# A fused encoder layer: which projection steps run beside the loading of x, and who spreads the cosines

## The chip, the cores and the metric

The kernel runs on one Trainium2 chip. Its eight cores run the same program, each on one element of the batch (2048 rows of 1024 channels), with no exchange between them. The metric is the device time of the slowest core, in microseconds (us). Engines are named PE (TensorE, matmuls and transposes), ACT (ScalarE), DVE (VectorE), POOL (GpSimd) and SP (SyncE, which here only issues DMAs). Each engine works through a queue of its own in program order; semaphores make it wait for others.

## The reference, cut to what matters

```python
h = rms_norm(x, norm_mix_pre)                      # 2048 x 1024, one norm per row
proj = h @ w_in
u_pool, q, k, v, g_pool, g_attn = split(proj)      # 512, 3 x 1536, 2 x 1024 channels
q, k = apply_rope(q, cos, sin), apply_rope(k, cos, sin)
for gi, (window, dil) in enumerate(((128, 1), (512, 4), (2048, 16))):
    o, lse = dilated_window_attention(q[g], k[g], v[g], dil, radius=64)   # 8 heads a group
# groups merged by softmax of lse; branch A: windowed means of u_pool
mix = (sigmoid(g_pool) * y_pool + sigmoid(g_attn) * y_attn) @ w_out
x = x + rms_norm(mix); x = x + rms_norm(SwiGLU(rms_norm(x)))
```

The change touches only the first lines: the norm of x, the projection to v and to q and k, and the rotation by cosine and sine.

## The kernel before, in words

**Tiles of x.** x comes in 16 tiles of 128 rows (512 KB each), over SP's queue into a ring of six buffers (`xring`). For tile i, `p1_s1` issues the load, `p1_s1b` squares the tile on ACT with a sum per row and makes 1/rms by a Ln and an Exp on one column, `p1_s2` multiplies on DVE by 1/rms and by the gain row g0 (one SCALAR_TENSOR_TENSOR, bf16 out, ring `hbf` of three), `p1_s3` transposes it with eight PE instructions into one bank of PSUM, and `p1_s4` copies the bank on DVE into hT. `p1_iter(t)` is one turn of this pipeline: in turn t the later stages come first, for tiles t-3, t-2 and t-1, then the square of tile t, then the load of tile t+5.

**Steps of projection.** After each `p1_iter(t)` the program puts up to 9 units of projection on PE (`run(9.0, ...)`), taken from the list `ready` when their turn has come (`pro(t)`). A step is 8 units. A v step (`v_step(w, n2)`) makes two 128-row tiles of v for the slab w: 16 matmuls of 256 columns against the weights `Wv[w % 2]`, one ACT copy out. Slab w holds 256 channels of v of head group w % 3. A q or k step (`qk_step(u, m, tb)`) makes 512 rows of q or k for unit u: 8 matmuls of 512 columns, then DVE multiplies the bank by the sines into bf16 and by the cosines in place, PE adds the rotated part with one more 512-column matmul about 11 units later, and ACT copies the result out (one copy for q, two for k). Before the change, `ready` holds the eight v steps of slab 0 and the eight q and k steps of unit 0. All sixteen are emitted by the end of the pipeline, behind turn 19.

**Then the attention.** 160 attention groups follow, each with a score step, an Exp, a mask multiply and a value step. Between them `pace(i)` says how many units of further projection (the list `jobs`, sorted by due group) are emitted per group: 18.4 for each of the first 14 groups.

**The other queues.** POOL fills constants in memory (`vones`, `kzero`), issues the weight loads that convert float32 to bf16 (`issue_v`, `issue_qk`) and, before the change, copies cosine and sine rows, which arrive in 32 partitions, over to the other 96 (eight copies of 1024 float32 columns, the line L622). Its waits on tiles of x (`tk._waits("pool", ...)`) hold back the weight loads. SP issues the loads of x and the constants; before it issues tile i it waits for tile i-3 to have landed, and for the buffer to be free.

The tables of order below name PE's rows so: L176 is a transpose, L170 with 128x256 a matmul of a v step, L173 a matmul of 512 columns of a q or k step, L170 with 128x512 the rotation.

## Time and profile before

| | us |
|---|---|
| median of 3 runs | 1144.59 (1143.5 to 1144.81) |
| profiled execution | 1146.5 |
| its span, slowest core (core 3) | 1145.0 |
| spans of the eight cores | 1139.3 to 1145.0 |
| PE busy in the span | 1084.6 (95%) |
| DVE, ACT, POOL busy | 523.2, 474.7, 96.2 |

The span runs from the first to the last instruction of a core; the profiled execution's time is 1.5 us longer than it. A timeline row says when a merged row of instructions starts, how long it takes, and in brackets how long the engine sat idle before it and which event ended that. A row of a stretch gives the stretch, its length, the busy time and number of instructions of PE, PE's weight loads, DVE, ACT and POOL, then the TensorE clock that was granted (1.00 is full speed), the busy share of the DMA engines and the GB/s that they moved. Of the DMA queues, q1 (hardware) is SP's and q0 (software) POOL's. A busy PE is not always a fast PE: the same instruction can take longer at a lower clock, so durations are compared too.

### The profile page before, as it was taken

To read this page: it belongs to the slowest core of one execution; us is meant where nothing else is said; L and a number is where in the kernel's file an instruction comes from. 1 tells how busy PE (TensorE), PEld (TensorE's weight loads), DVE (VectorE), ACT (ScalarE), POOL (GpSimd) and SP (SyncE) were. 2 spreads that over 40 slices of the span, in tenths; PEclk is the share of its full clock that TensorE was granted. 3 is DMA by queue.
4 is the path that set the end of the run, shared out by engine and by line. 5 is a ranking of instruction groups with operands and counts; after the bars stand their busy time and mean duration, and the time that the engine had idled before them with its cause. 6 is when DMAs were issued, how large, how long until landed. Compare 5 with 4: busy or idle time off the path is not lost.

```text
span 1145.0 us, 19739 instructions; the slowest of 8 cores (1139.3 to 1145.0 us)
## 1 busy us (share of the span) xinstructions
PE 1084.6 (95%) x6896; PEld 591.3 (52%) x6896; DVE 523.2 (46%) x817; ACT 474.7 (41%) x904; POOL 96.2 (8%) x181
## 2 busy tenths in 40 slices
PE   2799998989999999999999999999999999999995
PEld 1586564557665696444444444444444444444442
DVE  3835567765557765443436777212112111222221
ACT  3744476577565666322224878211111111211111
POOL 5620000000000000002000000111111000000000
PEclk9899999999999999999999999999999999999998
DMA  8852211121121403716004741554545210333321
GB/s 216 213 88 38 37 20 19 20 38 20 20 47 21 65 2 58 147 19 92 1 1 145 242 142 61 92 75 75 81 77 79 39 19 1 111 111 110 111 92 56
DMA packets 32017, 83.07 MB, mean 73 GB/s; under 512 B 4016, under 2 KB 4272, under 8 KB 31792
## 3 DMA queue, kind: packets, MB, share of 16 engines
q0 software_dynamic: 18768, 36.31, 20.7%
q1 hardware_dynamic: 13152, 45.49, 12.0%
q8 instruction: 58, 0.95, 0.3%
q14 instruction: 39, 0.32, 0.1%
HBM read 101.32 MB, written 16.78 MB: 103 GB/s over the span
## 4 chain that ended last, share of the span: by engine, by line
PE 81%; ACT 6%; DVE 6%; issue 4%; DMA 2%; ACTq 0%; DVEq 0%; SPq 0%; POOL 0%
PE ps L173 67%; PE ps L170 13%; ACT arena L184 6%; DVE arena L187 2%; DMA arena<-x 2%; DVE arena L190 2%; DVE arena L201 1%; ACT arena L255 1%; DVE ps L187 0%; PE ps L176 0%; DVE arena L197 0%; ACTq L68 0%; DVEq L68 0%; ACT L255 0%; ACT arena L592 0%
## 5 line engine op out<-in xcount | busy, mean ns | idle before, releaser
L173 PE MATMUL ps<-arena 128*128 128x512 bf16 (+2 forms) x4304 | 925.3, 368 | 9.7 <-ACT arena L184 4.5
L173 PEld LDWEIGHTS ps<-arena 128*128 128x128 bf16 x4304 | 412.6, 98 | 472.0 <-issue 17.3
L184 ACT ACTIVATE arena<-ps 128x512 bf16<-128x512 f32 (+5 forms) x578 | 352.6, 619 | 611.5 <-PE ps L173 498.0
L187 DVE TENSOR_TENSOR arena<-ps,arena 128x512 bf16<-128x512 f32 (+3 forms) x332 | 223.8, 677 | 433.7 <-PE ps L173 326.8
L170 PE MATMUL ps<-arena 128*128 128x256 bf16 (+5 forms) x2336 | 220.5, 239 | 7.6 <-DVE ps L187 3.2
L170 PEld LDWEIGHTS ps<-arena 128*128 128x128 bf16 x2336 | 168.4, 105 | 30.0 <-issue 12.9
L187 DVE TENSOR_TENSOR arena<-arena 128x512 bf16<-128x512 bf16 (+2 forms) x208 | 108.2, 524 | 78.7 <-ACT arena L184 69.6
L184 ACT ACTIVATE arena<-arena 128x1 f32<-128x1 f32 (+3 forms) x161 | 86.0, 538 | 36.8 <-DMA arena<-x 15.8
L190 DVE SCALAR_TENSOR_TENSOR arena<-arena 128x1024 bf16<-128x1024 f32 (+2 forms) x49 | 63.1, 1290 | 24.5 <-ACT arena L184 21.0
L187 DVE TENSOR_TENSOR ps<-ps,arena 128x512 f32<-128x512 f32 x96 | 67.2, 700 | 10.3 <-DVE arena L187 0.5
L176 PE MATMUL ps<-arena 128*128 128x128 bf16 x256 | 21.9, 235 | 29.8 <-DVE arena L190 28.7
L176 PEld LDWEIGHTS ps<-arena 128*128 128x128 bf16 x256 | 17.8, 105 | 37.9 <-issue 34.9
L201 DVE CAST arena<-ps 128x256 bf16<-128x256 f32 (+1 forms) x54 | 28.5, 528 | 10.2 <-PE ps L170 6.9
L210 POOL DMA_DIRECT2D arena<-w_fg x22 | 12.1, 549 | 216.3 <-PE ps L173 216.3
L197 DVE TENSOR_SCALAR arena<-arena 128x1 f32<-128x1 f32 (+1 forms) x28 | 7.5, 268 | 46.7 <-ACT arena L184 46.7
L210 POOL DMA_DIRECT2D arena<-w_qk x24 | 12.8, 537 | 160.8 <-PE ps L170 101.5
L190 DVE SCALAR_TENSOR_TENSOR arena<-ps,arena 128x1024 f32<-128x1024 f32 x16 | 20.5, 1280 | 6.2 <-ACT arena L184 6.1
L210 POOL DMA_DIRECT2D arena<-w_gt x16 | 8.5, 530 | 165.6 <-PE ps L173 96.0
L368 POOL MEMSET arena<- 64x2048 bf16 x8 | 14.4, 1798 | 0.9
L210 POOL DMA_DIRECT2D arena<-w_fu x22 | 11.8, 537 | 21.3 <-PE ps L173 21.3
L253 POOL MEMSET arena<- 128x1 f32 x32 | 2.4, 138 | 130.7 <-DVE arena L190 121.6
L195 DVE TENSOR_SCALAR arena<-ps,arena 128x512 bf16<-128x512 f32 x16 | 11.8, 743 | 0.3
(25 smaller groups left out, 96.3 us busy)
## 6 DMA issues: line engine op xcount, KB each, us to landing
arena<-x SPq DMA_DIRECT2D x32, 512.0 KB, 5.3
y<-arena SPq DMA_DIRECT2D x31, 512.0 KB, 2.9
arena<-y SPq DMA_DIRECT2D x16, 512.0 KB, 4.2
arena<-w_qk POOLq DMA_DIRECT2D x24, 256.0 KB, 4.1
arena<-w_fg POOLq DMA_DIRECT2D x22, 256.0 KB, 4.2
arena<-w_fu POOLq DMA_DIRECT2D x22, 256.0 KB, 5.4
arena<-w_fd POOLq DMA_DIRECT2D x11, 512.0 KB, 7.9
arena<-w_gt POOLq DMA_DIRECT2D x16, 256.0 KB, 4.3
```

The lines of the kernel that those rows point to most:

```text
L170: tk.op("pe", lambda e: e.matmul(out, lhsT=lhsT, rhs=rhs, start=start, stop=stop, skip_group_check=True), reads, writes, mark)
L173: tk.op("pe", lambda e: e.matmul(out, lhsT=lhsT, rhs=rhs, start=start, stop=stop), reads, writes, mark)
L176: tk.op("pe", lambda e: e.transpose(out, in_, ident), reads, writes, mark)
L184: tk.op("act", lambda e: e.activation(out=out, in_=in_, func=func, **kw), reads, writes)
L187: tk.op(eng, lambda e: e.tensor_tensor(out=out, in0=in0, in1=in1, op=op), reads, writes)
L190: tk.op("dve", lambda e: e.scalar_tensor_tensor(out=out, in0=in0, scalar=scalar, in1=in1, op0=op0, op1=op1), reads, writes)
L195: tk.op("dve", lambda e: e.tensor_scalar(out=out, in0=in0, scalar1=s1, scalar2=None, op0=op0), reads, writes)
L197: tk.op("dve", lambda e: e.tensor_scalar(out=out, in0=in0, scalar1=s1, scalar2=s2, op0=op0, op1=op1), reads, writes)
L201: tk.op("dve", lambda e: e.tensor_copy(out=out, in_=in_), reads, writes)
L210: tk.dma(qeng, key, lambda e: e.dma_start(out=out, in_=in_), reads, writes)
L255: tk.op("act", lambda e: e.activation(out=st[:, 1:2], in_=st[:, 0:1], func=AF.Ln, bias=epsb, scale=1.0 / D), (r, "epsb"), (r,))
L368: tk.op("pool", lambda e, o_=KT[s_][h_][z, :]: e.memset(o_, 0.0), (), (("Kz", s_), "pms"))
```

## The change

It does these things, all ahead of or within the loading of x:

1. The gain row is loaded into 32 partitions instead of 128, and two DVE copies spread it. Tile 0 of x is the first DMA that SP issues; the constants c_pk come third instead of first. The cosine and sine rows are asked for behind tile 9 instead of tile 3.
2. Up to four tiles of x are in flight instead of three (tile i waits for tile i-4). Turn t now holds the stages of tiles t-4, t-3 and t-2, and the square of tile t; each stage but the square is one turn later.
3. From tile 4 on, one Ln and one Exp serve two tiles. The square's unused output goes to a buffer of its own (`sqj`) instead of into `hbf`.
4. `ready` holds the v steps of slabs 0 and 1 while x is loading; q and k steps of unit 0 come from turn 17 on. Slab 1 (group 1, dilation 4) stores its tiles of v by row range first, so that two steps are possible from every four tiles of x; the value step of the attention reads them at the new place (`nv`).
5. DVE instead of POOL spreads the cosines, two copies in each of the turns 13 to 16. POOL asks for the weights of slab 0 behind tile 2 (was 1), of slab 1 behind tile 4 (was 14), of unit 0 behind tile 10 (was 3).
6. The eight v steps of slab 1 are gone from `jobs`, and `pace` gives 14.0 units for each of the first 14 groups.

```diff
         def after_x(i):
             if i == 0:
-                DMA("sp", "c2", g0, gains[0:1, :].partition_broadcast(128), writes=("g0",))
-            if i == 3:
+                DMA("sp", "c2", g0[0:32, :], gains[0:1, :].partition_broadcast(32), writes=("g0",))
+                DMA("sp", "c0", f32v(O_SM, 128), c_pk[:, 0:128], writes=("smbf",))
+            if i == 9:
...
         def p1_s1(i):
-            if i >= 2:
-                tk._waits("sp", tk._deps((("xr", max(i - 3, 0) % 6),), ()))
+            if i >= 4:
+                tk._waits("sp", tk._deps((("xr", (i - 4) % 6),), ()))
...
         def p1_s1b(i):
-            ACT(hbf[i % 3], xring[sl], AF.Square, ...)
+            ACT(sqj, xring[sl], AF.Square, ...)
+            a = i
+            if i >= 4:
+                if i % 2 == 0:
+                    return
+                a = i - 1
...
-        P1 = (p1_s1b, p1_s2, p1_s3, p1_s4)
-        for i in range(5):
+        P1 = ((0, p1_s1b), (2, p1_s2), (3, p1_s3), (4, p1_s4))
+        for i in range(6):
             p1_s1(i)
+        for n_ in (32, 64):
+            VCOPY(g0[n_:2 * n_, :], g0[0:n_, :], reads=("g0",), writes=("g0",))
...
-            ready = sorted([(2 * n2 + 5, 0, n2, f_) for n2, f_ in enumerate(w_steps(0))] +
-                           [(4 * (n_ % 4) + 8, 1, n_, f_) for n_, f_ in enumerate(u_steps(0))])
+            ready = sorted([(2 * n2 + 6, 0, n2, f_) for n2, f_ in enumerate(w_steps(0))] +
+                           [(4 * (n2 // 2) + 8, 1, n2, f_) for n2, f_ in enumerate(w_steps(1))] +
+                           [(max(4 * (n_ % 4) + 9, 17), 2, n_, f_) for n_, f_ in enumerate(u_steps(0))])
...
+                if 13 <= t < 17:
+                    q_ = t - 13
+                    for n_ in (32, 64):
+                        c_ = arena[:, O_CS + q_ * 1024:O_CS + (q_ + 1) * 1024]
+                        VCOPY(c_[n_:2 * n_, :], c_[0:n_, :], reads=(("cs", q_),), writes=(("cs", q_),))
...
-            add(w_steps(1), 0, 4)
...
-                    return 18.4
+                    return 14.0
```

PE at the start of the program, before: four transposed tiles, a v step, and then, from tile 6 on, v steps and q or k steps by turns between the tiles.

```order
L176 MATMUL ps<-arena 128x128 x32
L170 MATMUL ps<-arena 128x256 x16
L176 MATMUL ps<-arena 128x128 x16
L170 MATMUL ps<-arena 128x256 x16
L176 MATMUL ps<-arena 128x128 x8
L173 MATMUL ps<-arena 128x512 x9
L176 MATMUL ps<-arena 128x128 x8
L173 MATMUL ps<-arena 128x512 x7
L170 MATMUL ps<-arena 128x512
L170 MATMUL ps<-arena 128x256 x4
L176 MATMUL ps<-arena 128x128 x8
L170 MATMUL ps<-arena 128x256 x12
```

PE at the same place in the changed kernel:

```order
L176 MATMUL ps<-arena 128x128 x32
L170 MATMUL ps<-arena 128x256 x16
L176 MATMUL ps<-arena 128x128 x16
L170 MATMUL ps<-arena 128x256 x18
L176 MATMUL ps<-arena 128x128 x8
L170 MATMUL ps<-arena 128x256 x18
L176 MATMUL ps<-arena 128x128 x8
L170 MATMUL ps<-arena 128x256 x18
L176 MATMUL ps<-arena 128x128 x8
L170 MATMUL ps<-arena 128x256 x10
L176 MATMUL ps<-arena 128x128 x8
```

From the seventh tile on, each tile of transposes is followed by 18 or 10 matmuls of v steps, and none of a q or k step. Of the first x18, 16 matmuls belong to slab 0 and the last two to slab 1.

PE in the changed kernel around the last two tiles (the two L176 rows are the transposes of tiles 14 and 15), to the first q and k steps:

```order
L170 MATMUL ps<-arena 128x256 x18
L176 MATMUL ps<-arena 128x128 x8
L170 MATMUL ps<-arena 128x256 x18
L176 MATMUL ps<-arena 128x128 x8
L170 MATMUL ps<-arena 128x256 x12
L173 MATMUL ps<-arena 128x512 x16
L170 MATMUL ps<-arena 128x512
L173 MATMUL ps<-arena 128x512 x10
L170 MATMUL ps<-arena 128x512
```

All q and k steps of unit 0 stand behind the last tile's transposes.

DVE in the turns of the cosines; before, one turn with a q or k step in it and the next ones (the second row is the multiply for tile 11):

```order
L201 COPY arena<-ps 128x8x128 [waits pe]
L190 SCALAR_TENSOR_TENSOR arena<-arena 128x1024 [waits x5,act]
L187 TENSOR_TENSOR arena<-ps,arena 128x512 [waits pe,pool]
L187 TENSOR_TENSOR ps<-ps,arena 128x512 [waits dve]
L201 COPY arena<-ps 128x8x128
L190 SCALAR_TENSOR_TENSOR arena<-arena 128x1024 [waits x0,act]
L187 TENSOR_TENSOR arena<-ps,arena 128x512 [waits pe]
L187 TENSOR_TENSOR ps<-ps,arena 128x512 [waits dve]
```

and in the changed kernel (the first row is the multiply for tile 11, the 32x1024 and 64x1024 copies are the cosines):

```order
L190 SCALAR_TENSOR_TENSOR arena<-arena 128x1024 [waits x5,dve]
L201 COPY arena<-arena 32x1024 [waits c40]
L201 COPY arena<-arena 64x1024 [waits dve]
L201 COPY arena<-ps 128x8x128 [waits pe]
L190 SCALAR_TENSOR_TENSOR arena<-arena 128x1024 [waits x0,act]
L201 COPY arena<-arena 32x1024 [waits c41]
L201 COPY arena<-arena 64x1024 [waits dve]
L201 COPY arena<-ps 128x8x128 [waits pe]
L190 SCALAR_TENSOR_TENSOR arena<-arena 128x1024 [waits x1]
```

The multiplies by sine and cosine (TENSOR_TENSOR) have left the turns of the tiles, and two copies stand in each of four turns.

POOL, from its first fill on, before:

```order
L360 MEMSET arena 128x32x64
L368 MEMSET arena 64x2048 [waits pool] x2
L210 DMA arena<-w_v 128x2048 [waits x1]
L210 DMA arena<-w_qk 128x1024 [waits x3]
L210 DMA arena<-w_qk 128x1024
L622 COPY arena<-arena 32x1024 [waits c40,pool]
L622 COPY arena<-arena 64x1024 [waits pool]
L622 COPY arena<-arena 32x1024 [waits c41,pool]
```

and now:

```order
L368 MEMSET arena 128x32x64
L368 MEMSET arena 128x32x64 [waits pool]
L376 MEMSET arena 64x2048 [waits pool] x2
L210 DMA arena<-w_v 128x2048 [waits x2]
L376 MEMSET arena 64x2048 [waits pool] x2
L210 DMA arena<-w_v 128x2048 [waits x4]
L376 MEMSET arena 64x2048 [waits pool] x4
L210 DMA arena<-w_qk 128x1024 [waits x4]
L210 DMA arena<-w_qk 128x1024
L210 DMA arena<-w_qk 128x1024 [waits x2]
```

The load of slab 1 stands behind the landing of tile 4 (the second wait on x4 is that of tile 10, in the same buffer), and the copies of cosines are gone.

## Rows read from the trace of the kernel before

**Rows 1.** Spans of the cores, and the granted clock of each
```profile
core 1: 1139.3 us, clock 0.995
...
core 3: 1145.0 us, clock 0.992
```

**Rows 2.** Stretches of core 3, with busy times, clock, DMA share and GB/s
```profile
5.00:8.00 3.00, 0.00 (x0) 0.00 (x0) 0.00 (x0) 0.00 (x0) 1.70 (x1) 1.00 1.05 374
8.00:14.00 6.00, 1.06 (x9) 0.85 (x10) 2.77 (x3) 3.29 (x8) 0.66 (x1) 1.00 0.89 237
14.00:22.00 8.00, 1.97 (x16) 1.47 (x16) 3.79 (x4) 3.30 (x8) 2.92 (x4) 1.00 1.03 242
22.00:30.00 8.00, 4.72 (x32) 3.62 (x32) 3.22 (x5) 3.41 (x9) 7.22 (x7) 0.91 0.93 219
30.00:36.00 6.00, 3.97 (x28) 3.25 (x29) 5.47 (x5) 3.60 (x9) 5.64 (x4) 0.56 0.83 263
80.00:100.00 20.00, 20.00 (x152) 13.02 (x151) 9.36 (x16) 7.78 (x14) 1.06 (x2) 1.00 0.24 40
```

**Rows 3.** Timeline of core 3, TensorE: start, duration, instruction, idle before and releaser
```profile
23.07 2.90 PE L170 MATMUL ps<-arena 128*128 128x256 bf16 x16
...
32.84 3.13 PE L170 MATMUL ps<-arena 128*128 128x256 bf16 x16
...
45.36 1.91 PE L170 MATMUL ps<-arena 128*128 128x256 bf16 x16
47.11 0.61 PE L176 MATMUL ps<-arena 128*128 128x128 bf16 x8
47.56 2.11 PE L173 MATMUL ps<-arena 128*128 128x512 bf16 x9
49.50 0.61 PE L176 MATMUL ps<-arena 128*128 128x128 bf16 x8
...
60.81 0.61 PE L176 MATMUL ps<-arena 128*128 128x128 bf16 x8
```

**Rows 4.** The same view of core 1
```profile
20.73 3.57 PE L170 MATMUL ps<-arena 128*128 128x256 bf16 x16 [1.22 <-DMA arena<-w_v]
...
54.96 0.61 PE L176 MATMUL ps<-arena 128*128 128x128 bf16 x8
```

**Rows 5.** Waits of core 3 in 0 to 62 us: total, times, longest
```profile
PE ps L176 <- DVE arena L190: 27.9, 10, 11.7
```

**Rows 6.** Timeline of core 3, ScalarE: square of tile 4, all of tile 5
```profile
24.93 1.06 ACT L184 ACTIVATE arena<-arena 128x1024 bf16<-128x1024 f32 x1 [4.53 <-DMA arena<-x]
...
28.06 1.06 ACT L184 ACTIVATE arena<-arena 128x1024 bf16<-128x1024 f32 x1 [1.30 <-DMA arena<-x]
29.02 0.19 ACT L184 ACTIVATION_READ_ACCUMULATOR arena<-arena 128x1 f32 x1
29.30 0.29 ACT L308 ACTIVATE arena<-arena 128x1 f32<-128x1 f32 x1
29.68 0.20 ACT L184 ACTIVATE arena<-arena 128x1 f32<-128x1 f32 x1
```

**Rows 7.** DMAs issued in 8 to 14 us, core 3: size, us to landing
```profile
arena<-w_v POOLq DMA_DIRECT2D x1, 512.0 KB, 11.7
```

**Rows 8.** DMA queues in 14 to 22 us: packets, MB, share
```profile
q1 hardware_dynamic: 426, 1.41, 69.3%
q0 software_dynamic: 141, 0.52, 34.0%
```

**Rows 9.** ScalarE by form, 0 to 62 us: count, busy, mean ns
```profile
L184 ACT ACTIVATE arena<-ps 128x512 bf16<-128x512 f32 x8 | 4.8, 597 | 4.6 <-PE ps L170 4.5
```

**Rows 10.** Groups of VectorE by form, whole span
```profile
L190 DVE SCALAR_TENSOR_TENSOR arena<-arena 128x1024 bf16<-128x1024 f32 x32 | 42.4, 1326 | 19.6 <-ACT arena L184 19.6
...
L201 DVE COPY arena<-ps 128x1024 bf16<-128x1024 bf16 x16 | 10.9, 680 | 0.0
L197 DVE TENSOR_SCALAR arena<-arena 128x512 f32<-128x512 f32 x12 | 5.0, 420 | 2.2 <-ACT arena L184 2.2
```

More of the change, by code:

```diff
@@ L306, in p1_s1b @@
             r = ("st1", i)
-            ACT(hbf[i % 3], xring[sl], AF.Square, reads=(("xr", sl), r), writes=(("hbf", i % 3), r), accum_out=st1[:, 0, i:i + 1])
-            tk.op("act", lambda e: e.activation(out=st1[:, 1, i:i + 1], in_=st1[:, 0, i:i + 1], func=AF.Ln, bias=epsb, scale=1.0 / D),
-                  (r, "epsb"), (r,))
-            ACT(st1[:, 2, i:i + 1], st1[:, 1, i:i + 1], AF.Exp, reads=(r,), writes=(r,), scale=-0.5)
+            ACT(sqj, xring[sl], AF.Square, reads=(("xr", sl), r), writes=("sqj", r), accum_out=st1[:, 0, i:i + 1])
+            a = i
[3 more added lines that the diff above has]
+                a = i - 1
+            rr = tuple(("st1", q_) for q_ in range(a, i + 1))
+            tk.op("act", lambda e: e.activation(out=st1[:, 1, a:i + 1], in_=st1[:, 0, a:i + 1], func=AF.Ln, bias=epsb, scale=1.0 / D),
+                  rr + ("epsb",), rr)
+            ACT(st1[:, 2, a:i + 1], st1[:, 1, a:i + 1], AF.Exp, reads=rr, writes=rr, scale=-0.5)
         def p1_s2(i):
@@ L328, in p1_s4 @@
             VCOPY(hT[:, :, i * 128:(i + 1) * 128], pb, reads=(("ps", k),), writes=(("hT", i),))
-        P1 = (p1_s1b, p1_s2, p1_s3, p1_s4)
-        for i in range(5):
+        P1 = ((0, p1_s1b), (2, p1_s2), (3, p1_s3), (4, p1_s4))
+        for i in range(6):
             p1_s1(i)
+        for n_ in (32, 64):
+            VCOPY(g0[n_:2 * n_, :], g0[0:n_, :], reads=("g0",), writes=("g0",))
         def p1_iter(t):
-            for stg in reversed(range(4)):
+            for stg, fn in reversed(P1):
                 if 0 <= t - stg < NT:
-                    P1[stg](t - stg)
-            if t + 5 < NT:
-                p1_s1(t + 5)
+                    fn(t - stg)
+            if 6 <= t + 4 < NT:
+                p1_s1(t + 4)
         HT_ALL = tuple(("hT", i) for i in range(NT))
@@ L610, in grp_step, with wait_x @@
                 yield 1.0
+            def wait_x(i):
+                tk._waits("pool", tk._deps((("xr", i % 6),), ()))
             vones(0)
+            vones(1)
             kzero(0)
-            tk._waits("pool", tk._deps((("xr", 1),), ()))
+            wait_x(2)
             issue_v(0)
-            tk._waits("pool", tk._deps((("xr", 3),), ()))
-            issue_qk(0)
-            for q_ in range(4):
-                for n_ in (32, 64):
-                    src = arena[0:n_, O_CS + q_ * 1024:O_CS + (q_ + 1) * 1024]
-                    dst = arena[n_:2 * n_, O_CS + q_ * 1024:O_CS + (q_ + 1) * 1024]
-                    tk.op("pool", lambda e, o_=dst, i_=src: e.tensor_copy(out=o_, in_=i_), (("cs", q_),), (("cs", q_), "pms"))
@@ L628, in pro @@
             def pro(t):
                 return ready.pop(0)[3] if ready and ready[0][0] <= t else None
-            for t in range(NT + 4):
+            for t in range(NT + 5):
                 p1_iter(t)
                 clock[0] += 2.0
-                run(9.0, lambda: pro(t))
-                if t == 15:
-                    tk._waits("pool", tk._deps((("xr", 14 % 6),), ()))
-                    issue_v(1)
+                if 13 <= t < 17:
[3 more added lines that the diff above has]
+                        VCOPY(c_[n_:2 * n_, :], c_[0:n_, :], reads=(("cs", q_),), writes=(("cs", q_),))
+                run(9.0, lambda: pro(t))
+                if t == 10:
+                    wait_x(10)
+                    issue_qk(0)
+                if t == 14:
+                    wait_x(14)
@@ L638, in _rest @@
                     issue_qk(1)
-                    kzero(2)
-                    kzero(3)
                     issue_qk(2)
@@ L653, in _rest @@
             tk.inherit(tuple(("oat", j, hh) for j in range(4) for hh in range(2)),
-                       tuple(("hbf", i) for i in range(3)) + ("g0",))
+                       tuple(("hbf", i) for i in range(3)) + ("g0", "sqj"))
             def qwin(g, n):
```

16 lines of the change are left out of this document (10 added, 6 removed).

## The prediction, made before the changed kernel ran

> **What bounds the kernel now.** I read the spans of the cores first. The slowest, core 3, ends 5.7 us behind core 1 [rows 1], though both run the same program. Then I looked for a place in the two timelines of PE where the cores differ and after which they don't: the transposes of the last tile of x start at 60.81 us on core 3 [rows 3] and at 54.96 on core 1 [rows 4]. That is 5.85 apart, the whole difference. So the loading of x decides which core is slowest, and it is this stage that the change rewrites.
>
> How much of that stage is lost? I count what PE has executed ahead of tile 15, by the order of before: 15 tiles of transposes, 96 matmuls of v steps, 41 of q and k steps, 4 rotations. Full-speed prices come from start-to-start distances on core 3: a v step of 16 matmuls 47.11 - 45.36 = 1.75 (0.109 each), a tile's transposes 47.56 - 47.11 = 0.45, and 9 matmuls of 512 columns 49.50 - 47.56 = 1.94 (0.216 each) [rows 3]. Sum: 15 x 0.45 + 96 x 0.109 + 45 x 0.216 = 6.75 + 10.5 + 9.7 = 27.0 us. Lost before tile 15: 60.81 - 27.0 = 33.8 us on core 3, 28.0 on core 1. This "loss" (PE idle, or slower than full speed) is the quantity that the change can alter: the matmuls of the whole program stay the same in number and shape, and from tile 15 on PE has no gap to speak of (20.00 busy of 20.00 between 80 and 100 us [rows 2]).
>
> What makes the loss has two parts. Until 30 us it is DMA: the engines are 89 to 105% busy and move 374, 237, 242 and 219 GB/s in the four stretches to 30 us [rows 2], and ACT starts the squares of tiles 4 and 5 only when they land, at 24.93 and 28.06 [rows 6]. Behind that, PE waits for the multiply of DVE ahead of its transposes, 27.9 us in ten waits over the stage [rows 5], because sine and cosine multiplies stand in DVE's queue between the tiles. Core 3 was also granted less clock between 22 and 36 us (a mean of 0.91 and 0.56, from 2.4 GHz down to the 1.2 GHz level in part of it), after stretches with PE busy 1.97 of 8 and 4.72 of 8 us [rows 2]; its second v step took 3.13 us there instead of 1.91 [rows 3].
>
> **The change part by part.** The order of the changed kernel has 15 tiles of transposes and 180 v matmuls ahead of tile 15: 6.75 + 180 x 0.109 = 26.4 us of full-speed work. So I need the time T at which tile 15's transposes start; the new loss is T - 26.4. Two paths lead to T on core 3.
>
> *The DMA path.* What has to be moved until x15 has landed: 16 tiles of 0.524 MB (8.39), gains into 32 rows 0.13 (was 0.52), c_pk 0.06, cosines 0.52, the slabs 0 and 1 0.52 each, the weights of unit 0 0.52: 10.67 MB. From 8 to 30 us before moved 6 x 0.237 + 8 x 0.242 + 8 x 0.219 = 5.1 MB in 22 us, 0.232 MB/us, with full engines [rows 2]. At that rate, less 1.8 us for the 3 us at 374 GB/s, and starting at 4 to 5 us as before, x15 lands at 4.5 + 46 - 1.8 = 48.7. By queue, 1.41 MB of SP took 69.3% of 8 us, 3.9 us per MB, and 0.52 MB of POOL 34.0%, 5.2 us per MB [rows 8]; 9.1 x 3.9 + 1.57 x 5.2 = 43.7, so 48.2 without the faster start and 46.4 with it. From landing to transposes: tile 5 took 1.82 from the start of its square to the end of its Exp (28.06 to 29.88 [rows 6]), the multiply takes 1.33 [rows 10], and I add 0.3 for hand-overs, 3.5 in all. T is 50 to 52 by this path.
>
> *The PE path.* PE's queue now has the first two matmuls of slab 1 ahead of tile 6, and everything behind them is in order. Slab 1 is asked for when tile 4 has landed. The five tiles, gains, c_pk and parts of slab 0 and tile 5 are some 3.4 MB, which at before's pace (1.1 MB in 5 to 8 us [rows 2] and about 0.25 earlier, then 0.232 per us) is 16.8 us, against 24.93 before. A load of v took 11.7 us from issue to landing in that crowd [rows 7]; so PE starts at 28.5, or, if the 5.4 MB up to slab 1 are counted instead, at 25.5. I take 27. Done by then: 6 tiles and 32 matmuls, 2.7 + 3.5 = 6.2 us. Left until tile 15: 20.2. T = 47.2 with no stall.
>
> Stalls on that path. ACT per two tiles: 2 x (1.06 + 0.19) + 0.29 + 0.20 [rows 6], two copies of v at 0.60 [rows 9], 4.2 us, where PE needs 4.4 (64 matmuls and four tiles are 8.8 per four turns): just hidden. With a Ln and an Exp for each tile it would be 4.7 and not hidden, 0.3 per two tiles over five pairs, so the pairing is worth about 1.5 us, already in the 47.2. DVE per tile: multiply 1.33 + copy 0.68 [rows 10], 2.0, hidden. In the four turns 13 to 16 it also has two cosine copies. The trace has no such copy on DVE. From below stands the nearest float32 operation with one input, 0.42 for 512 columns; from above the two-input one at 1.33 for 1024 [rows 10]. I take 0.7, nearest to the first, as the one-input form is about half as costly per column. Four turns are then 4 x (2.0 + 1.4) = 13.6 against PE's 8.8, 4.8 too long, less what the multiplies run ahead of PE, which I put at most of one turn, 1.8: 3 us. With 0.42 it is 1, with 1.33 about 8. If the DMA path is late anyway, part of it hides there. One slow v step more at the start, 3.13 - 1.91 = 1.2. PE path: T = 51.4.
>
> The Trainium skill (VectorE: DVE Perf Modes, "The perf-mode tier table") says that a float32 copy in SBUF runs at 2x, a tensor_tensor at 1x. By its fixed 151 cycles and 0.96 GHz a copy of 1024 would be an estimated 0.69 us, and the sum as above; at 1x the other end. The 0.42 of the 512-column row agrees with 2x.
>
> I take T = 50.7 on core 3: loss 24.3, gain 33.8 - 24.3 = 9.5. On core 1, whose first v step waited for its slab until 20.73 [rows 4] against 23.07, DMA is about 3 us ahead: T = 47.7 to 48.5, loss 21.7, gain 6.3.
>
> The rest. *POOL's eight copies* vanish; POOL was waited for by nothing that paces. *c_pk third*: its transposes need it only after tile 0; nothing. *g0 by two copies*: 1.4 us on DVE beside tile 0's square and statistics (1.8 [rows 6]), behind a quarter of the bytes; hidden, and it ends in DMA time anyway. *Cosines asked for behind tile 9*: SP's four issues delay tile 10 by about 2.4 us, with three tiles in flight; hidden unless DMA idles. *issue_qk(0) behind tile 10*: landing near 45, needed behind tile 15; if it came 10 us late PE would wait 3. *Unit 0 behind tile 15*, then unit 1: sixteen q and k steps nearly in a row; 1.4 of DVE per 1.95 of PE, hidden, bounded by -1 to +2 us. *Slab 1 out of jobs, 14.0 for 18.4*: 64 units less over 14 groups is 4.6 per group; neither gain nor loss beyond 1 us.
>
> Sum against the profiled execution: 1145.0 - 9.5 = 1135.5 of span, 1137.0 with the 1.5 around it. The runs shown have a median 1.9 below that execution, so their slowest core had not quite core 3's bad start; I give them the mean of 9.5 and 6.3, 8.0: 1144.6 - 8.0 = 1136.6.
>
> **The rivals.** (a) *The crowd is thinner than I think.* Landing of slab 1 at 24 and no stall by the cosines: T = 45 to 46, gain 13 to 14, 1131. For it: DMA moved 374 GB/s for a while [rows 2]. Against: 10.67 MB still have to come. The Trainium skill (DMA: Bandwidth & Descriptors, "Queues, rings and completion order") has each DMA engine take turns between queues, packet by packet, so a slab would get half the rate beside x and land in about 4.5 us once it starts. Here q0 moved 141 packets against 426 of q1 in 8 us, a quarter [rows 8]: not that.
>
> (b) *DVE takes PE's place.* Cosine copies at 1.33, or turns that were hidden by less than I think: 5 us more, gain 3, 1141.5. For it: DVE is what PE waits for now [rows 5]. Against: 0.42 [rows 10].
>
> (c) *DMA was the bound and stays it*: with two slabs ahead of x the rate falls to 0.2 MB/us, x15 lands near 55, T = 58, loss 32: gain 2, within the noise, 1142.5 to 1144. Against: between 30 and 36 us 263 GB/s with 83% [rows 2].
>
> (d) *Slower: the slab gates x.* Slab 1's two matmuls stand ahead of tile 6. While they wait, no transposes run, hbf's three buffers fill, the multiplies stop, x's ring fills and the loads stop. Then T = (landing of slab 1) + 20.2 + 4.2. It equals the old loss at T = 60.2, so from a landing at 35.8 on the change loses. A slab that takes twice 11.7 us lands at 40: 4 us slower, 1149. Four tiles in flight instead of three speak for it, the order in which bytes are asked for against it.
>
> **How the numbers follow.** Forecast 62%; (a) 13%, (b) 11%, (c) 7%, (d) 7%. The range takes in (a) to its middle, the bounds of the copies and most of (b): 1131.5 to 1142. A measurement here tells about 0.2%, 2.3 us, from no change. Faster by more: forecast, (a), (b) and a little of (c), 0.86; within, most of (c): 0.08; slower 0.06.
>
> **What would show it.** After: tile 15's transposes near 50 on the slowest core; the square of tile 5 before 22 us; the first x18 row waiting for DMA of w_v until 25 to 29; cosine copies of about 0.7; 263 GB/s or so until the end of x; no sine multiply before tile 15; and spans of the cores nearer to each other. Wrong if PE's sum of waits for the multiply stays near 27.9 past 25 us, if tile 15 starts later than 54, or if gaps appear between 60 and 120 us.

## The result, and the profile after

The changed kernel took 1141.38 us (median of 8 runs) against 1145.09 for the kernel before on the same chip, a ratio of 0.9967 with a 95% interval of 0.9955 to 0.9978. So it is faster by 3.7 us, 0.3%, where I forecast 8.0 and gave 1131.5 to 1142.0 as the range; the forecast gain was more than twice the measured one. One of the eight runs, with four cores at a lower granted clock (0.88 to 0.90), took 1250.2 and is not in the ratio. The profiled execution took 1141.0, its slowest core 1139.5.

The spans of the cores, as in [rows 1]: all eight now end between 1138.1 and 1139.5. Core 3 gained 5.9 us, core 1 only 1.2.

```profile
core 1: 1138.1 us, clock 0.996
...
core 3: 1139.1 us, clock 0.995
...
core 7: 1139.5 us, clock 0.995
```

The stretches of [rows 2] on core 3:

```profile
5.00:8.00 3.00, 0.00 (x0) 0.00 (x0) 1.21 (x1) 1.61 (x4) 2.88 (x2) 1.00 0.97 289
8.00:14.00 6.00, 2.02 (x16) 1.55 (x16) 5.61 (x6) 4.46 (x12) 3.50 (x4) 1.00 0.99 294
14.00:22.00 8.00, 3.06 (x22) 2.31 (x23) 6.08 (x7) 4.00 (x9) 7.61 (x6) 1.00 0.98 223
22.00:30.00 8.00, 7.06 (x63) 5.98 (x62) 3.52 (x4) 4.02 (x11) 1.45 (x1) 1.00 1.02 250
30.00:36.00 6.00, 6.00 (x68) 5.54 (x67) 4.54 (x6) 4.49 (x9) 1.05 (x2) 1.00 1.03 336
80.00:100.00 20.00, 19.00 (x125) 10.62 (x124) 14.23 (x23) 10.09 (x18) 4.40 (x4) 1.00 0.43 61
```

The reader sees the transfers run as full as before, PE busy earlier (7.06 of 8 us between 22 and 30, where it was 4.72), and a granted clock of 1.00 in every stretch. Matmuls at the very start are slow all the same: the first v step below took 3.57 us for 16 matmuls, where 1.91 is usual [rows 3]. That is about half the pace at a granted clock of 1.00, and what causes it stays open; core 1 had the same 3.57 before [rows 4]. Between 80 and 100 us PE now has two small waits of about 0.5 us, where it had none (one of them, for ACT, was there before at 74.55); the rest of the program is nonetheless about as long as before, as shown below. PE's timeline, to set beside [rows 3]:

```profile
20.96 3.57 PE L170 MATMUL ps<-arena 128*128 128x256 bf16 x16 [3.41 <-DMA arena<-w_v]
...
25.54 2.13 PE L170 MATMUL ps<-arena 128*128 128x256 bf16 x18
...
35.56 2.13 PE L170 MATMUL ps<-arena 128*128 128x256 bf16 x18
...
47.24 0.61 PE L176 MATMUL ps<-arena 128*128 128x128 bf16 x8 [1.78 <-DVE arena L190]
...
50.78 0.61 PE L176 MATMUL ps<-arena 128*128 128x128 bf16 x8 [0.97 <-DVE arena L190]
...
54.20 0.61 PE L176 MATMUL ps<-arena 128*128 128x128 bf16 x8 [0.85 <-DVE arena L190]
```

The first row is the first v step, which waits 3.41 us for slab 0. The second is the second step with the first two matmuls of slab 1 behind it, the third such a row further on (2.13 us for 18 matmuls, at full speed). The last three rows are the transposes of tiles 13, 14 and 15. Tile 15 starts at 54.20, where the forecast had 50.7. Between tiles 13, 14 and 15 lie 3.54 and 3.42 us, though PE has only 2.4 us of work per tile; in each case it waits for the multiply of DVE. The sum of PE's waits up to 62 us, beside [rows 5]:

```profile
PE ps L176 <- DVE arena L190: 19.1, 9, 11.6
...
PE ps L170 <- DMA arena<-w_v: 3.4, 1, 3.4
```

Of the 19.1 us (27.9 before), 11.6 are the wait for tile 0 and 1.8 the two ahead of tiles 2 and 3; 5.6 lie behind 25 us, 3.6 of them ahead of tiles 13 to 15 in the rows above. What DVE does in these last turns, on core 7, the slowest: two cosine copies (one row, x2), the tile copy, the multiply, and again.

```profile
47.99 1.47 DVE L201 COPY arena<-arena 32x1024 f32<-32x1024 f32 x2
49.49 0.69 DVE L201 COPY arena<-ps 128x1024 bf16<-128x1024 bf16 x1
50.10 1.28 DVE L190 SCALAR_TENSOR_TENSOR arena<-arena 128x1024 bf16<-128x1024 f32 x1
51.41 1.47 DVE L201 COPY arena<-arena 32x1024 f32<-32x1024 f32 x2
52.91 0.69 DVE L201 COPY arena<-ps 128x1024 bf16<-128x1024 bf16 x1
53.52 1.28 DVE L190 SCALAR_TENSOR_TENSOR arena<-arena 128x1024 bf16<-128x1024 f32 x1
```

and PE beside it:

```profile
48.10 0.61 PE L176 MATMUL ps<-arena 128*128 128x128 bf16 x8 [1.84 <-DVE arena L190]
...
51.52 0.61 PE L176 MATMUL ps<-arena 128*128 128x128 bf16 x8 [0.85 <-DVE arena L190]
```

DVE's rows follow one another without a gap, every 3.42 us (47.99, 51.41, ...), and a tile's transposes start right after a multiply ends. Two cosine copies take 1.47, so one is 0.735; the forecast had 0.7.

How far back does this chain reach? On core 3 (DVE for tiles 10 and 14, ACT for tile 15):

```profile
37.11 1.28 DVE L190 SCALAR_TENSOR_TENSOR arena<-arena 128x1024 bf16<-128x1024 f32 x1 [1.54 <-ACT arena L184]
...
45.17 1.06 ACT L184 ACTIVATE arena<-arena 128x1024 bf16<-128x1024 f32 x1 [1.61 <-DMA arena<-x]
...
46.80 0.20 ACT L184 ACTIVATE arena<-arena 128x2 f32<-128x2 f32 x1
...
49.36 1.28 DVE L190 SCALAR_TENSOR_TENSOR arena<-arena 128x1024 bf16<-128x1024 f32 x1
```

DVE waits for the last time ahead of the multiply of tile 10, at 37.11. From there its queue runs without a wait, and tile 15's transposes start 17.1 us later (17.0 to 17.2 on all eight cores). The last tile of x is not part of this chain. Its square starts at 45.17, as soon as it has landed, and the Exp for tiles 14 and 15 ends at 47.00; but DVE reaches the multiply of tile 14 only at 49.36, 2.4 us later (2.2 to 3.4 over the cores). So in the changed kernel the transfers are done in time, and DVE is late.

One pair of numbers describes every kernel of this study: T, the start of tile 15's transposes, and the rest, a core's span less its T. Before, T is 54.96 to 60.81 over the eight cores (mean 56.97) and the rest 1084.2 to 1084.5. In the changed kernel T is 53.35 to 54.95 (mean 54.25) and the rest 1084.2 to 1084.9 (mean 1084.6 for 1084.3). The start of tile 6's transposes went from 29.95 to 35.80 (eight cores) to 28.61 to 29.75. From tile 6 to tile 15 it was 25.0 us on most cores before and is 24.0 to 25.6 after: nothing was won there. So, by these numbers, the change made the late cores as early as the good ones, and little more.

### The profile page after: what moved, and what is told of

Read it like the earlier page. It is cut to its first block, busy times and chain, and to the rows that moved or that the text cites. A ratio compares the mean times of both kernels' runs of the same rounds, so it can differ in the third digit from the quotient of the medians.

```text
span 1139.5 us, 19711 instructions; the slowest of 8 cores (1138.1 to 1139.5 us)
## 1 busy us (share of the span) xinstructions
PE 1084.6 (95%) x6896; PEld 590.0 (52%) x6896; DVE 532.1 (47%) x827; ACT 471.2 (41%) x892; POOL 87.7 (8%) x173
## 4 chain that ended last, share of the span: by engine, by line
PE 79%; DVE 7%; ACT 6%; issue 4%; DMA 2%; ACTq 0%; DVEq 0%; SPq 0%; POOL 0%; POOLq 0%
PE ps L173 67%; PE ps L170 12%; ACT arena L184 6%; DVE arena L190 3%; DMA arena<-x 2%; DVE arena L187 2%; DVE arena L201 1%; ACT arena L255 0%; DVE ps L187 0%; DVE arena L197 0%; ACTq L68 0%; DVEq L68 0%; ACT L255 0%; SPq L210 0%; ACT arena L600 0%
## 5 line engine op out<-in xcount | busy, mean ns | idle before, releaser
L173 PEld LDWEIGHTS ps<-arena 128*128 128x128 bf16 x4304 | 412.8, 98 | 472.8 <-issue 17.2
L184 ACT ACTIVATE arena<-arena 128x1 f32<-128x1 f32 (+4 forms) x155 | 84.3, 550 | 29.8 <-DMA arena<-x 9.8
L176 PE MATMUL ps<-arena 128*128 128x128 bf16 x256 | 21.2, 231 | 20.3 <-DVE arena L190 19.5
L176 PEld LDWEIGHTS ps<-arena 128*128 128x128 bf16 x256 | 17.4, 104 | 27.6 <-issue 25.2
L201 DVE COPY arena<-ps 128x1024 bf16<-128x1024 bf16 x16 | 11.0, 687 | 6.0 <-PE ps L176 5.8
```

What stands on the lines that cost most here:

```text
L173: tk.op("pe", lambda e: e.matmul(out, lhsT=lhsT, rhs=rhs, start=start, stop=stop), reads, writes, mark)
L176: tk.op("pe", lambda e: e.transpose(out, in_, ident), reads, writes, mark)
L184: tk.op("act", lambda e: e.activation(out=out, in_=in_, func=func, **kw), reads, writes)
L201: tk.op("dve", lambda e: e.tensor_copy(out=out, in_=in_), reads, writes)
```

## The experiments

Each was taken in turn with the kernel before on one chip, which gives the ratio. The chip was not the same for all: e_late, e_pool, e_third and e_unpair ran on one, e_late2, a_oldsteps, b_oldfront and p_early on a second, e_mix, p_three and p_gains on a third. So between groups the ratios are compared, and where their intervals overlap no difference is claimed. All numbers of T and of the rest are read from the eight cores' timelines of one profiled execution.

| kernel | median us | ratio to before (95%) | T, mean (lowest to highest) | rest, mean |
|---|---|---|---|---|
| changed kernel | 1141.4 | 0.9967 (0.9955 to 0.9978) | 54.2 (53.4 to 55.0) | 1084.6 |
| e_late | 1142.7 | 0.9977 (0.9966 to 0.9988) | 50.5 (49.3 to 51.6) | 1088.4 |
| e_pool | 1138.3 | 0.9938 (0.9924 to 0.9951) | 50.6 (49.8 to 51.7) | 1084.7 |
| e_third | 1144.2 (one run) | | 57.1 (56.1 to 58.7) | 1084.1 |
| e_unpair | 1141.4 | 0.9966 (0.9954 to 0.9978) | 53.9 (52.8 to 55.8) | 1085.1 |
| e_late2 | 1139.6 | 0.9947 (0.9933 to 0.9961) | 50.5 (49.1 to 52.7) | 1086.1 |
| a_oldsteps | 1145.3 | 0.9997 (0.9987 to 1.0007) | 57.4 (55.6 to 59.0) | 1084.1 |
| b_oldfront | 1145.7 | 0.9999 (0.9989 to 1.0009) | 53.2 (50.1 to 56.1) | 1086.7 |
| p_early | 1139.2 | 0.9943 (0.9927 to 0.9960) | 51.2 (49.5 to 52.9) | 1084.5 |
| e_mix | 1140.1 | 0.9955 (0.9941 to 0.9970) | 51.1 (49.6 to 52.4) | 1085.0 |
| p_three | 1141.0 | 0.9969 (0.9956 to 0.9982) | 52.4 (50.2 to 55.0) | 1084.5 |
| p_gains | 1138.7 | 0.9945 (0.9925 to 0.9965) | 51.6 (50.3 to 53.0) | 1084.0 |

**e_late: the copies behind the last tile.**

```diff
-                if 13 <= t < 17:
-                    q_ = t - 13
+                for q_ in {17: (0, 1), 18: (2,), 19: (3,)}.get(t, ()):
```

> The changed kernel, with the eight cosine copies moved out of the turns 13 to 16 into the turns 17 to 19, behind the last multiply of a tile. Theory D (DVE took PE's place: its queue of tile copy 0.68 + multiply 1.28 + two cosine copies 1.47 = 3.42 us per tile in four turns is the chain that leads to tile 15): without them PE goes on at 2.42 or 1.55 us per tile from the transposes of tile 12 on, tile 15's transposes start at 50.5 instead of 54.2 to 55 us, and the kernel takes 1137.5, that is 3.5 to 4.4 us less than the changed kernel's 1141.4 and about 0.9935 of the kernel before. Theory X (the loading of x and of the slabs is what the end of the stage waits for, DVE only fills the time): tile 15's transposes stay within 1 us of 54.5 and the time at 1141. Rival P (sixteen q and k steps in a row cost what was gained elsewhere): tile 15 earlier, but the time stays, with new gaps of PE between 55 and 120 us.

T fell by 3.7 us to the 50.5 that was expected, but the kernel got no faster: the rest grew by 3.8. The second half looks as rival P has it (tile 15 earlier, the time unchanged, a new gap of PE), but the cause is the place of the copies, not the row of q and k steps (e_pool, below, has the same row and no such gap). On core 2, PE from tile 15 on:

```profile
51.16 0.61 PE L176 MATMUL ps<-arena 128*128 128x128 bf16 x8
51.61 1.47 PE L170 MATMUL ps<-arena 128*128 128x256 bf16 x12
53.13 3.40 PE L173 MATMUL ps<-arena 128*128 128x512 bf16 x15
59.53 0.38 PE L170 MATMUL ps<-arena 128*128 128x512 bf16 x1 [3.00 <-DVE ps L187]
59.75 3.96 PE L173 MATMUL ps<-arena 128*128 128x512 bf16 x10
```

and DVE:

```profile
50.43 2.98 DVE L201 COPY arena<-arena 32x1024 f32<-32x1024 f32 x4
53.44 0.69 DVE L201 COPY arena<-ps 128x1024 bf16<-128x1024 bf16 x1
54.16 1.47 DVE L201 COPY arena<-arena 32x1024 f32<-32x1024 f32 x2
55.67 0.69 DVE L201 COPY arena<-ps 128x1024 bf16<-128x1024 bf16 x1
56.39 1.47 DVE L201 COPY arena<-arena 32x1024 f32<-32x1024 f32 x2
57.89 0.69 DVE L187 TENSOR_TENSOR arena<-ps,arena 128x512 bf16<-128x512 f32 x1
```

All eight copies and two tile copies stand ahead of the first multiply by sines (57.89). PE has finished the matmuls of the first two q or k steps (one of the 16 is missing in the records) and waits 3.00 us for it (2.98 to 3.01 on six of the others, 2.62 on core 5). The next ten matmuls took 3.96 us, where the same ten take 2.32 in e_late2, which has no such wait ahead of them. The granted clock of the next stretch is 0.83, part of it at the 1.2 GHz level, after a stretch with PE busy 6.95 of 10 us. That is some 3.4 us at half clock, not the 7 that the text ahead of e_late2 names. The slowing did not follow on every core: on cores 1, 5 and 7 the ten took 2.32 behind the same kind of wait, and their rest is 1086.9 to 1087.7, against 1088.8 to 1089.3 on the others.

```profile
50.00:60.00 10.00, 6.95 (x51) 4.69 (x50) 9.24 (x14) 1.19 (x2) 0.00 (x0) 1.00 0.93 137
60.00:70.00 10.00, 9.95 (x43) 4.50 (x43) 5.56 (x8) 3.07 (x6) 0.00 (x0) 0.83 0.02 4
```

**e_pool: the copies on GpSimd**, behind the weights of unit 0. The eight calls are those of before, put behind `issue_qk(0)`:

```diff
                 if t == 10:
                     wait_x(10)
                     issue_qk(0)
+                    for q_ in range(4):
+                        for n_ in (32, 64):
+                            src = arena[0:n_, O_CS + q_ * 1024:O_CS + (q_ + 1) * 1024]
+                            dst = arena[n_:2 * n_, O_CS + q_ * 1024:O_CS + (q_ + 1) * 1024]
+                            tk.op("pool", lambda e, o_=dst, i_=src: e.tensor_copy(out=o_, in_=i_), (("cs", q_),), (("cs", q_), "pms"))
```

> The changed kernel with the cosine copies back on GpSimd, behind the weights of unit 0. Theory D: tile 15 starts near 51; the four multiplies beside the GpSimd copies may take longer than 1.28 (up to 1.9, as some did before), which costs up to 1.5 of it; time 1138 to 1139.5. Theory X: no change, 1141. If GpSimd's copies cost DVE as much as its own, tile 15 stays at 54.

As theory D has it, and the lowest median of the study: T 50.6, the rest unchanged, 1138.3 us, 3.1 less than the changed kernel, and the intervals of the two ratios do not touch. PE on core 4, tiles 12 to 15 (the L176 rows):

```profile
43.78 0.61 PE L176 MATMUL ps<-arena 128*128 128x128 bf16 x8
...
45.32 0.61 PE L176 MATMUL ps<-arena 128*128 128x128 bf16 x8
45.77 2.13 PE L170 MATMUL ps<-arena 128*128 128x256 bf16 x18
49.29 0.61 PE L176 MATMUL ps<-arena 128*128 128x128 bf16 x8 [1.40 <-DVE arena L190]
49.73 2.13 PE L170 MATMUL ps<-arena 128*128 128x256 bf16 x18
51.70 0.61 PE L176 MATMUL ps<-arena 128*128 128x128 bf16 x8
```

Tile 15 follows 14 after 2.41 us: PE sets the pace again, with one wait of 1.40. Two things are in that wait: DVE waits 1.59 us for ACT ahead of the multiply of tile 14, and the multiply itself takes 2.11 us instead of 1.28 beside the GpSimd copies:

```profile
41.58 1.28 DVE L190 SCALAR_TENSOR_TENSOR arena<-arena 128x1024 bf16<-128x1024 f32 x1 [0.19 <-ACT arena L184]
...
43.38 1.46 DVE L190 SCALAR_TENSOR_TENSOR arena<-arena 128x1024 bf16<-128x1024 f32 x1
...
47.03 2.11 DVE L190 SCALAR_TENSOR_TENSOR arena<-arena 128x1024 bf16<-128x1024 f32 x1 [1.59 <-ACT arena L184]
...
49.66 1.27 DVE L190 SCALAR_TENSOR_TENSOR arena<-arena 128x1024 bf16<-128x1024 f32 x1
```

The wait for ACT is the landing of the last tile of x. On core 3, ACT for tile 15 and DVE for tile 14:

```profile
44.58 1.06 ACT L184 ACTIVATE arena<-arena 128x1024 bf16<-128x1024 f32 x1 [0.63 <-DMA arena<-x]
...
46.59 1.28 DVE L190 SCALAR_TENSOR_TENSOR arena<-arena 128x1024 bf16<-128x1024 f32 x1 [1.27 <-ACT arena L184]
```

The same wait of DVE stands there on all eight cores of e_pool and of e_late (0.73 to 1.74 us), and on none of the changed kernel. On seven of the eight the square before it had waited for the tile. So without the cosine copies the transfers set T, at about 50.5; with them DVE does, at 54.2.

**e_third: one copy more per quarter.**

```diff
-                    for n_ in (32, 64):
+                    for n_ in (32, 64, 64):
```

> The changed kernel with the second cosine copy of each quarter made twice: 12 copies instead of 8, four more of about 0.74 us on DVE in turns 13 to 16. Theory D: each adds its full length, tile 15's transposes start 2.9 us later, at 57 to 58, and the spans grow by as much, to about 1142. Theory X: at most 1 us later.

T went from a mean of 54.2 to 57.1: 2.9 us for four copies, each its full 0.73. DVE is the chain in these turns; 1144.2 is a single run, and the slowest core's span of 1142.6 is near the 1142 expected.

**e_unpair: a Ln and an Exp for each tile**, without the block that joins two.

```diff
-            if i >= 4:
-                if i % 2 == 0:
-                    return
-                a = i - 1
```

> The changed kernel with a Ln and an Exp for every tile again. My prediction counted 1.5 us for the pairing. Theory D: ScalarE is not on the chain behind turn 12, where DVE sets the pace, so the time is within 0.5 us of 1141.4; an odd tile's multiply may even start no later and an even tile's earlier, since it needn't wait for the next square. If ScalarE is the bound: 1.5 us slower, 1143.

The same time, 1141.4. ScalarE isn't the bound in the changed kernel, and the 1.5 us that I gave the pairing are worth nothing there. (What it is worth where DVE isn't the bound wasn't tried.)

**e_late2: the copies where DVE is free.**

```diff
+                for q_ in {17: (0, 1), 20: (2,)}.get(t, ()):
...
+            for n_ in (32, 64):
+                c_ = arena[:, O_CS + 3072:O_CS + 4096]
```

The added loop at the end copies the fourth quarter, ahead of `run(1000.0, ...)`.

> The changed kernel with the cosine copies spread where DVE had no other work in the run before: the first two quarters behind the last multiply of a tile (turn 17), the third behind the first q step's multiplies, the fourth behind the second's. In e_late all eight stood ahead of the first q step's multiplies, PE waited 3.0 us for them and ran 7 us at half clock behind that. Theory D, refined (a copy costs PE its full length wherever DVE's next result is what PE waits for, and nothing where DVE idles): tile 15 at 50.5 as in e_late, and the span behind it back from 1087 to 1089 to 1084.5 us; kernel 1138.0. If the copies cost the same anywhere: 1141.

Half right: T as expected, but 1139.6 and not 1138.0. The rest is 1086.1, 1.4 above e_pool's. The copies between the first q steps' multiplies still let PE wait, 0.50 and 0.93 us on core 2: per step DVE has 1.4 us of multiplies to 1.95 of PE, and a quarter's 1.47 does not fit into what is left.

**a_oldsteps and b_oldfront: the two halves of the change.** The first has the new loading with the steps of before; its `ready` is

```diff
-                           [(4 * (n2 // 2) + 8, 1, n2, f_) for n2, f_ in enumerate(w_steps(1))] +
-                           [(max(4 * (n_ % 4) + 9, 17), 2, n_, f_) for n_, f_ in enumerate(u_steps(0))])
+                           [(4 * (n_ % 4) + 9, 1, n_, f_) for n_, f_ in enumerate(u_steps(0))])
```

with weights, cosines, jobs and pace as before.

> The changed kernel's loading (x first, gains into 32 rows, four tiles in flight, stages one turn later, Ln and Exp for two) with the steps of before: slab 0 and unit 0 beside x, slab 1 in the jobs at 18.4 units a group, cosines behind tile 3 and copied by GpSimd, weights asked for as before. Theory F (the front of the loading removed the late start of the slow cores, the steps did nothing for it): tile 6's transposes near 29.5 on all cores, none at 33 to 36, and from tile 6 to tile 15 25 us as before, since DVE has the sine and cosine multiplies again: 1141. Theory S (what made some cores late was the weights of unit 0 and the cosines asked for early): the spread of tile 6 (30 to 36) comes back here, 1144 to 1145.

No gain: 1145.3. Tile 6 at 30.3 to 33.6, so the latest cores are earlier than before (35.8) and the early ones later; and from tile 6 to 15 25 us again, with the multiplies by sine and cosine in DVE's queue. Neither theory had all of it: the time is that of theory S, the 25 us that of theory F, and the spread is smaller, not gone, and not back.

The second is e_pool with the old `p1_s1`, `p1_s1b`, `P1`, `p1_iter` and order of c_pk and gains:

```diff
-                DMA("sp", "c2", g0[0:32, :], gains[0:1, :].partition_broadcast(32), writes=("g0",))
-                DMA("sp", "c0", f32v(O_SM, 128), c_pk[:, 0:128], writes=("smbf",))
+                DMA("sp", "c2", g0, gains[0:1, :].partition_broadcast(128), writes=("g0",))
...
+        DMA("sp", "c0", f32v(O_SM, 128), c_pk[:, 0:128], writes=("smbf",))
```

> The other half: only value steps beside x as in the changed kernel, with the cosine copies on GpSimd (as in e_pool), but the loading of before: c_pk first, gains into 128 rows, three tiles in flight, Ln and Exp for each tile, the square into hbf, stages one turn earlier. Compare e_pool, 1138.3. Theory F: tile 6 is late on some cores (to 33 or more) and the kernel 2 to 5 us slower than e_pool. Theory S: tile 6 within 1 us of e_pool's 29.3 on all cores; from tile 6 to 15 then tells what the later stages and the pairing are worth: e_pool has 21.2 us, and I expect 22 to 24 here, since a tile's chain of square, Ln, Exp and multiply has one turn less.

No gain either: 1145.7. In this kernel only 162 v matmuls stand ahead of tile 15, so its T is to be compared with e_pool's after adding 18 x 0.109 = 2.0: 52.1 to 58.0 against 49.8 to 51.7. The steps alone leave some cores late, from tile 12 on instead of at tile 6 (core 3: 44.99 to 55.51 from tile 12 to tile 15, 10.5 us where PE has 6.4 of work). There the square of tile 14 waited 2.29 us for x, until 47.70, and the 18 matmuls behind it took 3.64 us instead of 2.13.

So the halves are not additive: neither alone gives a measurable gain, both together with the copies on GpSimd 0.6%. An explanation that fits, argued and not tested by itself: value steps take DVE's load out of the turns, so that x becomes what is waited for; the new loading brings x sooner, which is of no use while DVE's queue holds the pace of 25 us.

**p_early, p_three, p_gains: what of the loading matters.** All are e_pool with one edit.

p_early asks for the slabs earlier:

```diff
             vones(0)
-            vones(1)
-            kzero(0)
-            wait_x(2)
+            wait_x(0)
             issue_v(0)
-            kzero(1)
-            wait_x(4)
+            vones(1)
+            kzero(0)
+            wait_x(2)
             issue_v(1)
+            kzero(1)
```

p_three has three tiles in flight instead of four:

```diff
-            if i >= 4:
-                tk._waits("sp", tk._deps((("xr", (i - 4) % 6),), ()))
+            if i >= 2:
+                tk._waits("sp", tk._deps((("xr", max(i - 3, 0) % 6),), ()))
```

p_gains asks for 128 rows of gains and has no copies of them:

```diff
-                DMA("sp", "c2", g0[0:32, :], gains[0:1, :].partition_broadcast(32), writes=("g0",))
+                DMA("sp", "c2", g0, gains[0:1, :].partition_broadcast(128), writes=("g0",))
...
-        for n_ in (32, 64):
-            VCOPY(g0[n_:2 * n_, :], g0[0:n_, :], reads=("g0",), writes=("g0",))
```

> e_pool with the slabs' weights asked for two tiles earlier: slab 0 behind tile 0 instead of 2, slab 1 behind tile 2 instead of 4. In e_pool PE waits 3.3 to 4.8 us for slab 0, until 21 to 22.6 us. If that wait bounds the stage, tile 6 comes 2 to 3 us earlier (27) and the kernel is at 1136. If the loading of x itself does (then the slabs only take their bytes ahead of x), tile 6 stays within 1 us of 29.3, the wait for slab 0 turns into a wait for DVE ahead of tiles 4 to 6, and the time stays at 1138.

The second case: tile 6 no earlier (28.3 to 32.3), and 1139.2, not distinguishable from e_pool. PE no longer waits for slab 0 but for the multiplies of tiles 4 and 5 (3.54 us ahead of tile 4 on core 3).

> e_pool with three tiles of x in flight instead of four, all else the same. It tells what of the loading's gain (tile 6's transposes at 29.3 on all cores where b_oldfront has 25 to 30 and tile 15 on some cores at 55 to 56) is the fourth tile in flight. If it is: some cores late again at tile 15 (53 or more), kernel 1140 to 1142. If the later stages and the pairing do it: tile 15 at 50 to 51.7, 1138.3.

Three in flight cost 2.7 us of time and 1.9 of mean T, most on the latest core (55.0). The square of tile 15 starts at 46.5 on average over the cores, where it is 44.4 in e_pool, and on cores 0, 2 and 4 the square of tile 14 ahead of it waited 1.3 to 2.0 us for x. So x arrives later by about what T loses. b_oldfront, with all of the old loading, has a T 4.6 above e_pool's after the correction, so the fourth tile in flight is a good part of what the loading gained, not all.

> e_pool with the gain row loaded into all 128 partitions and without the two copies. In the changed kernel these copies took 3.2 to 4.1 us beside a GpSimd memset, where cosine copies of the same size took 1.47, and they hold the first multiply until 9.7 to 10.1. If that chain mattered, tile 6 is earlier here in spite of 0.39 MB more (1.5 us of transfers); if bytes matter more, tile 6 is 1 to 1.5 us later and the kernel at 1139 to 1140. If neither, 1138.3.

Between the cases: T 1.0 later, the rest 0.7 shorter, the time within noise of e_pool. The run changes the bytes and the copies together, so it does not price either. (On the eight cores of the changed kernel the two copies took 2.8 to 4.1 us.)

**e_mix: three quarters on GpSimd, one on DVE.**

```diff
+                for q_ in {17: (0,)}.get(t, ()):
...
+                    for q_ in (1, 2, 3):
+                        for n_ in (32, 64):
```

The second loop is on GpSimd, behind the w_pgrp loads of turn 14.

> The changed kernel with the first quarter of the cosines copied by DVE behind the last multiply of a tile (turn 17) and the other three by GpSimd, behind its weight loads of turn 14. e_pool's GpSimd copies ran beside the last multiplies (one took 2.11 us instead of 1.28), e_late2's DVE copies cost 1.5 us behind tile 15. Here both should go: tile 15 at 50.0 and the span behind it 1084.8, kernel 1137.3. If GpSimd's copies slow the multiplies by sine and cosine, or the second quarter lands too late for the second q step, the span behind tile 15 grows to 1086 and the time is e_pool's 1138.3 or more.

No gain over e_pool: 1140.1 where 1137.3 was expected, T 51.1 and the rest 1085.0. Whether it is slower is not shown, since the ratios' intervals overlap. DVE's two copies met GpSimd's six, as on core 2. GpSimd's timeline:

```profile
45.85 9.15 POOL L662 COPY arena<-arena 32x1024 f32<-32x1024 f32 x6
```

and DVE's:

```profile
51.23 2.87 DVE L201 COPY arena<-arena 32x1024 f32<-32x1024 f32 x2
```

Six copies took 9.15 us, 1.04 to 1.85 each, and the two on DVE 2.87 instead of 1.47 (2.86 or 2.87 on all eight cores).

## Why the prediction was wrong, point by point

**Right: the account.** The time that PE loses ahead of tile 15 is what differs between cores and between kernels. On core 3 the loss fell from 33.8 to 54.20 - 26.4 = 27.8, that is 6.0, and the span by 5.9. The rest is 1084.2 to 1084.5 before and 1084.2 to 1084.9 after; its mean grew by 0.3, though 0.6 us of PE's work moved into it (27.0 to 26.4 ahead of tile 15). So unit 0 behind tile 15, unit 1 right after it, and the 14.0 for 18.4 cost at most 0.5 us, within the bound given.

**Right in the number, in part by luck: the start of PE's path.** Slab 1's first two matmuls ran at 25.54 + 1.75 = 27.3 on core 3; the forecast was 27. But they did not wait for slab 1, which landed near 26 (asked for at 15.3 to 15.9, about 10.4 us to landing). What set their time was slab 0, for which PE waited until 20.96, and the slow first step. The sign "the first x18 row waiting for w_v" did not appear, and rival (d), this slab gating x, did not occur.

**Right in the number, by two errors that cancel: the path of transfers.** It was to give T = 50 to 52, and e_late and e_pool, where it does set T, have 50.5. But the square of tile 15 starts, at its landing on seven of eight cores, at 44.6 on average in e_late, not at 46.4 to 48.7, and from the start of its square to its transposes it took 5.8 us (core 3 of both kernels), not 3.5. With one Exp for two tiles, tile 14's multiply waits for tile 15's square too, so two multiplies stand behind the landing; the forecast counted one.

**Wrong: the step from "PE path: T = 51.4" to "I take T = 50.7", in its term for DVE's work.** The length of a copy was right (0.7, measured 0.735). The forecast took 4.8 us of surplus in turns 13 to 16, let 1.8 of it be absorbed by multiplies that run ahead of PE, kept 3, and then took 0.7 off because a late path of transfers might hide part. On core 3, from tile 11 to tile 15 PE needed 54.20 - 40.95 = 13.25 us for 8.8 of work: 4.5 lost where the forecast had 3. Another 2.1 were lost ahead of tiles 6 and 10, where the multiply waited for ACT; the forecast had nothing there but 1.2 for a slow v step, which lies before the 27.3. So 27.3 + 20.2 + 2.1 + 4.5 = 54.1, where 27 + 20.2 + 1.2 + 3 = 51.4 was forecast.

What the runs show in its place is a third path, DVE's own, which was not priced: from the multiply of tile 10 at 37.1 it runs 17.1 us without a wait, to 54.2. The path of transfers alone ends at 50.5 (e_late, e_pool). T is the later of the two. The eight copies are 5.9 us of work and cost 3.7, the distance between the two ends: the other 2.2 are hidden, because DVE would otherwise have waited for tile 15. Hiding was thus a right idea with a wrong amount, since the transfers were done earlier than forecast. Once DVE's path is the later one, more work on it costs its full length (e_third: 2.9 for four copies). That is rival (b), with 11%: its time of 1141.5 is the measured one, its second reason (hidden by less than I think) holds, its first (copies at 1.33) does not.

**Wrong: core 1.** I let its head start in transfers (called 3 us, though 23.07 - 20.73 is 2.3) live on to T = 48.1. Measured: 53.83. DVE's last wait ends between 36.3 and 37.9 on all cores of the changed kernel and the 17.1 us behind it are the same for all, so a good core had little to win: its start of tile 6 went from 29.95 to 29.47. My 8.0 was thus a mean of one gain 3.6 too large (9.5, measured 5.9) and one 5.1 too large (6.3, measured 1.2). Their mean, 4.4, is the miss in the gain (8.0 for 3.7); the other 0.5 between 1136.6 and 1141.4 is the median of the kernel before, 1145.1 here and 1144.6 when the forecast was made.

**A misreading on the way.** The 27.9 us of [rows 5] were put down to sine and cosine multiplies in DVE's queue. On core 3 before, 11.66 of them are the wait for tile 0, 7.6 more lie ahead of tiles 1 to 3, and 5.0 ahead of tiles 4 and 5, all before the first q or k step. Only 3.6 us, four waits behind 41 us, can be due to those multiplies. So there was less to win by taking them out, and "stays near 27.9 past 25 us" was a sign that could not appear: the kernel before has 8.7 there, the changed one 5.6. Of the other signs, tile 15 later than 54 did appear (54.2).

**Without effect: the pairing**, counted at 1.5 (e_unpair). What it costs or gives where the landing of tile 15 sets T was not tried. **The reduced clock** of core 3 before (0.56 between 30 and 36 us) is gone in the changed kernel; how much of its 5.9 us is clock was not separated.

**The rule on copies** from the Trainium skill (VectorE: DVE Perf Modes, "The perf-mode tier table") held: 0.69 estimated, 0.735 start to start. It says nothing of whether the copy is hidden.

**What stays open** is what made single cores late in the kernel before. It is gone only with both halves of the change; the fourth tile in flight is part of it. The medians moved by 3.7 us and the profiled executions by 5.5: the profiled execution of before, at 1146.5, is a late one among runs of 1143.5 to 1146.9, and the core that is slowest changes from run to run.

## What to carry to other kernels

When work moves to another engine, write down that engine's own chain to the event that everything waits for, from its last wait on, and set it beside the chain of the transfers. The later end counts: here 37.1 + 17.1 = 54.2 for VectorE against 50.5 for the landing of x, so that 5.9 us of copies cost 3.7. An average share of busy time shows neither. When statistics are shared by two tiles, count what both release behind the later one. And before a gain is forecast from the slowest core, ask what the fastest one would gain: where a change only makes the cores alike, the fast one tells the floor.
